# Sums of the squares of x over all eight feature tiles by one-column matmuls, in place of two folds on VectorE

## What is computed

```python
def rms_norm(x, g):
    x32 = x.astype(jnp.float32)
    y = x32 * lax.rsqrt(jnp.mean(x32 * x32, axis=-1, keepdims=True) + NORM_EPS)
    return (y * g.astype(jnp.float32)).astype(x.dtype)

for l in range(DEPTH):                                   # DEPTH = 2
    h = rms_norm(x, mix_pre_g[l]) * (1.0 + scale_m) + shift_m
    y = hybrid_mixer(h, ...)
    x = x + gate_m * rms_norm(y, mix_post_g[l])
    h = rms_norm(x, ffn_pre_g[l]) * (1.0 + scale_f) + shift_f
    y = conv_ffn(h, ...)
    x = x + gate_f * rms_norm(y, ffn_post_g[l])
```

## Time and profile before

| | us |
|---|---|
| median of 3 runs | 1294.04 |
| lowest and highest | 1292.98, 1294.46 |
| the profiled execution | 1294.48 |
| its span in the trace | 1292.6 |
| PE matmul busy | 1177.5 (91%) |
| VectorE busy | 855.9 (66%) |
| ScalarE busy | 536.7 (42%) |

### The profile page before, as it was taken

One profiled execution on the slowest core, in us unless ns is written; L12 is line 12 of the kernel. 1 busy time (PEld: TensorE's weight loads), 2 busy tenths in 40 slices (PEclk: granted clock), 3 DMA queues, 4 the chain that ended last, 5 costly groups with the idle time before them and its releaser, 6 DMA issues.

```text
span 1292.6 us, 15931 instructions
## 1 busy us (share of the span) xinstructions
PE 1177.5 (91%) x6534; PEld 1012.4 (78%) x6534; DVE 855.9 (66%) x1293; ACT 536.7 (42%) x756; POOL 56.6 (4%) x66
## 2 busy tenths in 40 slices
PE   5988859889899999999988986899999999999996
PEld 5876549788778888888988764888888888888895
DVE  6786877878776777777566866457864466445545
ACT  4265553445322442344334566344542244234430
POOL 1011130000000000000000023000000000000000
PEclk7989879899999999999999979899999999999998
DMA  9513136323576447743221312020433333333211
GB/s 363 215 61 113 49 114 204 140 79 134 179 244 228 147 147 239 240 147 122 82 67 41 107 33 82 1 98 1 147 99 98 98 98 98 98 97 94 94 58 66
DMA packets 44936, 155.76 MB, mean 121 GB/s; under 512 B 5056, under 2 KB 7360, under 8 KB 44864
## 3 DMA queue, kind: packets, MB, share of 16 engines
q1 hardware_dynamic: 44720, 154.23, 35.5%
q10 hardware_dynamic: 144, 0.52, 0.1%
HBM read 152.64 MB, written 2.10 MB: 120 GB/s over the span
## 4 chain that ended last, share of the span: by engine, by line
PE 65%; DVE 22%; ACT 7%; DMA 3%; issue 3%; SPq 0%; DVEq 0%; ACTq 0%
PE ps L1626 65%; DVE sb_wL L1019 3%; DMA sb_raw<-in_w 3%; DVE sb_y L1078 2%; DVE sb_xc L1255 1%; DVE sb_R L1357 1%; ACT sb_wH L586 1%; DVE sb_y L1304 1%; DVE sb_x L1082 1%; ACT sb_R L757 1%; ACT sb_sq L683 1%; DVE sb_stage L1025 1%; DVE sb_y L1101 1%; DVE sb_tiny L1220 1%; DVE sb_adaw L1025 1%
## 5 line engine op out<-in xcount | busy, mean ns | idle before, releaser
L1626 PE MATMUL ps<-sb_hH,sb_wH 128*128 128x512 f32 (+1 forms) x1184 | 425.5, 365 | 19.9 <-DVE sb_wL L1019 8.8
L1626 PE MATMUL ps<-sb_hH,sb_wL 128*128 128x512 f32 (+1 forms) x1184 | 418.9, 360 | 0.0
L1626 PE MATMUL ps<-sb_hL,sb_wH 128*128 128x512 f32 (+1 forms) x1184 | 397.4, 360 | 3.9 <-DVE sb_hL L1108 3.9
L1626 PEld LDWEIGHTS ps<-sb_hH,sb_wH 128*128 128x128 f32 x1184 | 229.4, 194 | 60.6 <-DVE sb_wL L1019 10.3
L1626 PEld LDWEIGHTS ps<-sb_hH,sb_wL 128*128 128x128 f32 x1184 | 229.2, 194 | 32.3
L1019 DVE TENSOR_TENSOR sb_wL<-sb_raw,sb_wH 128x1024 fp32r<-128x1024 f32 x174 | 212.8, 1228 | 58.9 <-ACT sb_wH L586 58.5
L586 ACT ACTIVATE sb_wH<-sb_raw 128x1024 fp32r<-128x1024 f32 x174 | 181.9, 1051 | 154.8 <-DMA sb_raw<-in_w 154.8
L1626 PEld LDWEIGHTS ps<-sb_hL,sb_wH 128*128 128x128 f32 x1184 | 215.4, 193 | 37.0 <-DVE sb_hL L1108 4.7
L1626 PE MATMUL ps<-sb_mL,sb_wH 128*128 128x256 f32 (+1 forms) x608 | 206.6, 340 | 20.6 <-DVE sb_mL L1313 20.3
L1626 PE MATMUL ps<-sb_mH,sb_wH 128*128 128x256 f32 (+1 forms) x608 | 206.0, 339 | 5.9 <-ACT sb_mH L923 5.2
L1626 PE MATMUL ps<-sb_mH,sb_wL 128*128 128x256 f32 (+1 forms) x608 | 204.6, 337 | 0.0
(11 more groups left out here) (230 smaller groups left out, 1144.5 us busy)
## 6 DMA issues: line engine op xcount, KB each, us to landing
sb_raw<-in_w SPq DMA_DIRECT2D x174, 512.0 KB, 3.7
sb_adaw<-in_ada SPq DMA_DIRECT2D x48, 512.0 KB, 4.4
sb_stage<-in_ada SPq DMA_DIRECT2D x24, 512.0 KB, 11.2
sb_vw<-in_ada SPq DMA_DIRECT2D x24, 512.0 KB, 4.2
sb_side<-in_w SPq DMA_DIRECT2D x8, 512.0 KB, 4.9
sb_raw<-in_w SPq DMA_DIRECT2D x8, 384.0 KB, 14.2
sb_x<-in_x SPq DMA_DIRECT2D x4, 512.0 KB, 5.2
out<-sb_x SPq DMA_DIRECT2D x4, 512.0 KB, 2.9
```

What stands on the lines that cost most here:

```text
L1626: return nc.tensor.matmul(out, a, b, start=start, stop=stop, **kw)
```

## The change

`x_sums` and its semaphore `x_summed` go, with the four places that call it (six executions). PE waits for the two squares themselves, and sums all eight feature tiles: for each 128 tokens eight matmuls on one column of ones accumulate, sixteen in all where there were four. Where `x_sums_mm` stands in PE's list is not changed, and nothing else moves.

```diff
-            def x_sums(l, k, h):
-
-                dve.wait_ge(xsq_ready, 2 * norm_half(l, k, h))
-                link(TT(xsq[0], xsq[0], xsq[1], ALU.add))
-                TT(xsq[0][:, 0:2 * HALF], xsq[0][:, 0:2 * HALF], xsq[0][:, 2 * HALF:], ALU.add).then_inc(x_summed, 1)
-
...
                 lo_chunk(U0 + 1)
-                x_sums(l, 0, 0)
                 lo_chunk(U0 + 2)
                 late(14, 2)
...
                 lo_chunk(U0 + 5)
-                x_sums(l, 0, 1)
                 x_recip(l, 0, 1)
...
                 lo_chunk(N0 + 3)
-                x_sums(l, 1, 0)
                 add_square(l, 1, 3, 1)
                 x_recip(l, 1, 0)
...
                 lo_chunk(N0 + 5)
-                x_sums(l, 1, 1)
                 x_recip(l, 1, 1)
...
             def x_sums_mm(l, k, h):
 
-                pe.wait_ge(x_summed, norm_half(l, k, h))
-                half_sums(h, 2, xsq[0]).then_inc(x_cols, 1)
+                pe.wait_ge(xsq_ready, 2 * norm_half(l, k, h))
+                for t in range(2):
+                    for j in range(KT):
+                        first = (j % 4) * HALF + t * P
+                        last = mm(bank(STAT_BANK[h])[:, 2 + t:3 + t], xsq[j // 4][:, first:first + P], ones[:, 0:1],
+                                  j == 0, j == KT - 1)
+                last.then_inc(x_cols, 1)
```

More of the change, by code:

```diff
@@ L286, in build @@
         post_rs, post_rb = sem("post_rs"), sem("post_rb")
-        x_half, xsq_ready, x_summed = sem("x_half"), sem("xsq_ready"), sem("x_summed")
+        x_half, xsq_ready = sem("x_half"), sem("xsq_ready")
         x_cols, x_sd, x_rs, x_rb = sem("x_cols"), sem("x_sd"), sem("x_rs"), sem("x_rb")
```

## The result

| | before, us | changed, us |
|---|---|---|
| median | 1294.25 (4 runs) | 1308.08 (4 runs) |
| lowest and highest | 1292.98, 1297.67 | 1305.94, 1309.98 |
| ratio, 95% interval | | 1.0105 [1.0087, 1.0123] |
| span of the profiled execution | 1292.6 | 1305.7 |

A forecast was written before the change was run, and what follows sets the result against it. PE, busy 91% of the span, was taken as the bound. Half 1 +7.5, the half 0 places -0.95, 0 and +1.4, and the clock +4.5 sum to +12.45 us: 1306.5 us against the median 1294.04, range 1299.5 to 1312.

The forecast's parts named there:

- Bound and places: Whole kernel: PE bounds it, 91% busy; it could win only its 6.9 us of fold waits, all at half 0.
- Price of a pass: Every place: 24 more passes cost PE 2.5 us, 3.4 us for all 32.
- the 3.3 to 3.6 us that the prediction wanted to see: Half 1: sign of being right, time from first pass to first product of chunk 5, before 0.91 us.
- The term of 2.5 us a place: Half 1, three places: the 24 added passes stand in front of the spread, +7.5 us in all.
- Half 1 on the path: Three half 1 places: PE never waits, so the added passes delay the spread, +7.5 us (ends +7.1 and +8.2).
- One sign: Half 1: VectorE's wait for the spread was to grow from 2.96 to above 6 us.
- First half 0: After the first mixer: VectorE's queue 1.9 us shorter, won time filled with products at half speed, -0.95 us.
- The far end, -1.9: Half 0 after the first mixer: the largest gain allowed, in us; the other end was 0.
- Second half 0: After the network of layer 0: passes just fill PE's wait, 0 us (ends -0.1 and +0.3).
- Third: Half 0 after the second mixer: passes start 1.06 us earlier but take 2.5 us more, +1.4 us.
- The clock: Half 1: passes act as a gap, the clock falls and chunk 5 loses 3 x 1.5 = +4.5 us.
- The sum, 12.45 us: Whole kernel: +7.95 us without the clock and +4.5 us for it, on the profiled execution's 1294.48.

The follow-up runs named there:

- e1: The changed kernel once more, with no edit; 1307.08 us, ratio 1.0096 on the kernel before.
- e2: Kernel before, folds kept, with 12 further one-column matmuls (24 passes) into an unused bank at each half 1; 1309.31 us, ratio 1.0105.
- e4: Changed kernel with the sixteen matmuls of each half 1 mixed into chunk 4, two ahead of each three products; 1320.46 us, ratio 1.0205 on the kernel before.
- e5: Kernel before with PE summing all eight tiles only at half 0 after the first mixer, folds kept elsewhere; 1292.06 us, ratio 0.9987.
- e9: Repeat of the kernel with PE summing all eight tiles only at half 0 after the first mixer; 1294.71 us, ratio 1.0002 on the kernel before.
- e3: Kernel before, folds kept, with 24 products of 256 columns into an unused bank at each half 1; 1304.91 us, ratio 1.0078.
- e6: Kernel before with PE summing all eight tiles at the three half 0 places, folds kept at half 1; 1295.75 us, ratio 1.0012.

## Why the prediction was right

- **Bound and places.** PE's 6.9 us of waits for the folds went to 0.3. The split into half 0 and half 1 decided: -0.5 us and +15.3 us.
- **Price of a pass.** 3.4 us for 32; measured 3.49 us where the clock was full, at four places (263.78 - 260.29 in the changed kernel, and all three of e1). At the other two half 1 places the clock fell inside the passes and they took 3.82 and 4.41 us. So two of three places in the changed kernel's trace lie outside the 3.3 to 3.6 us that the prediction wanted to see. The term of 2.5 us a place is 2.6 at full clock.
- **Half 1 on the path.** The stage was +2.55 us where no fall came (e1), and passes added with the folds kept make the whole loss (e2). One sign was read wrongly: VectorE's wait for the spread was to grow from 2.96 to above 6 us, and it was 4.47, 5.62 and 5.12 us. It starts at the reciprocal, which the passes put off as well (VectorE now waits 5.85 us for the root there, where it was 1.44), so only the longer chunk 5 adds to it.
- **First half 0.** The spread after the squares came 1.87 us earlier, at 239.81, as the 1.9 said, with the root (238.79 + 0.26) ahead of the reciprocal. Half of it was to be lost to the low clock. The stretch behind was 1 us longer than before in e1, e4 and e5, but not in the changed kernel's first trace nor in e9, and it was 1 us longer in e3 too, where the place is as before. So the two outcomes are seen, and that the change causes either is not. The far end, -1.9, was passed by 0.4 us in the first trace (-2.11 in the stage and -0.22 behind it).
- **Second half 0.** 0 forecast, +0.19 measured. **Third.** +1.4 forecast, +1.39 measured at the first product; in that trace another 1.04 us went behind it at the low clock, which I had left out. It is not steady: the stretch from there to the next second squares took 14.97 us before and 16.01 in the changed kernel, but 14.29 in e1, and 16.19 in e9, where this place keeps its folds.
- **The clock.** This is the term mis-sized most: forecast were 3 x 1.5 us. Chunk 5 lost 1.52, 2.32 and 2.15 us, and the passes themselves 0.33 and 0.92, as the low clock also reached into them: 7.6 us with the 0.4 us at the spread and the openings of the second place. In e1 it was 0, 1.5 and 1.5. The direction was argued from the start of the kernel, where passes did not bring the clock up; that was one place, and the products behind them ran at 0.50 for a while as well. e2 against e3 shows it: passes at this place bring the fall, products of 256 columns don't.

The Trainium skill (TensorE: Matmul & The Clock Gate, Part 1) sets the clock by how busy PE has lately been. The traces agree only if busy is not the busy column: 14 of 14 us of it went with 0.51. Its Part 4 says of transposes that they don't count as busy in the same way; no run here tests that, which makes it no more than a likeness to what one-column passes do.

The sum, 12.45 us, against 13.1 in the trace and 13.8 between the medians, is right partly by luck: 3.3 us more were lost at half 1 than forecast (15.3 against 12.0), and against that stood 1.0 us at half 0 (-0.5 against +0.45) and 1.7 us in stages that nobody touched.

## What to carry to other kernels

Moving a reduction from an idle engine to the engine that bounds the kernel can pay only where that engine waits. Here it shortened the stage at one place of six, where PE stood idle and VectorE's queue was the last to arrive; where the new work just filled PE's wait nothing was won, and where PE waited less than the new work takes, or not at all, time was lost. Look at each place by itself. Even at the good one the kernel was not surely faster.

A matmul of one column costs PE about 0.21 us here (2.58 us for twelve more; two passes, each with a fresh load of 128 columns). Price it also for what it does to the clock. In these runs passes between products made the products behind them slower, and mixing them in among products was worse than doing them in one go.

## What was not expected of the hardware

- With passes and products in turns the clock was at 0.51 for 14 us with PE never idle, the last 4 us of them in products alone (e4); against the changed kernel it lost 12 to 13 us by a change of order alone.
- The same 32 passes at the same place took 3.73 us or 6.18 us, by the moment at which the clock fell (e5, e6). Times of e6 spread over 10 us (1289.92 to 1299.59), those of the kernel before over 4.6 beside it (1292.3 to 1296.87).
